# Gate and up projections of feed-forward tiles 3 to 20 as seven block products each

## The chip, the cores and the metric
The kernel runs on one NeuronCore of one Trainium2 chip. The metric is device time in microseconds. Three runs of the kernel before took 2664.05, 2674.93 and 2677.69 us, median 2674.93.

## The reference, cut to what matters
Two equal layers are applied to 576 tokens (512 of a prompt, 64 of a sample). In each layer a feed-forward network stands first and another last; between them are a mixer of four head groups and a cross attention over 256 memory rows.

```
def swiglu(x, w_gate, w_up, w_down):
    return (jax.nn.silu(x @ w_gate) * (x @ w_up)) @ w_down

x = layer_norm(ALPHA * x + 0.5 * swiglu(x, ffn1_gate, ffn1_up, ffn1_down), g[0], b[0])
mix, state = parallel_mixer(x, ...)
x = layer_norm(ALPHA * x + mix, g[1], b[1])
x = layer_norm(ALPHA * x + cross_attention(x, mem_k, mem_v, x_wq, x_wo), g[2], b[2])
x = layer_norm(ALPHA * x + 0.5 * swiglu(x, ffn2_gate, ffn2_up, ffn2_down), g[3], b[3])
```
The model width is 1024, the hidden width 2816. All data is fp32.

## The kernel before
**Precision.** Every operand of a large product is split into a high part (rounded to fp32r, TensorE's one-pass fp32 kind) and a low part (the rest). A product takes three matmuls: high by high, high by low, low by high (`passes`, L394). One matmul is 128 weights columns by 288 tokens, half of the 576, into one PSUM bank. Both halves, h0 and h1, lie in the two banks of a "pair"; the pairs are A, B, D0 and D1.

**Weights.** All weights come as a stream of "units" of 128x1024 (512 KB), in the order of use. SyncE loads them into a ring of three raw buffers. Pool splits each: one TENSOR_SCALAR makes the high part (L2135), four TENSOR_TENSORs the low part (L2142), into one of 12 slots. `unit_split` counts units that are ready, `unit_done` units that TensorE is through with; `SLOT` and `BEFORE` say which slot a unit gets and which unit must be done first. RING is 3, so the load of a unit waits for the split of the unit three before it.

**A feed-forward network** has 22 hidden tiles of 128, each with a gate unit and an up unit, and down units for every two tiles. TensorE goes through it in four stretches:
- The head: tiles 0 to 2, all six units for half h0, then all six for h1 (96 matmuls for four of them and 24 for each of the other two), while the LayerNorm before it is still finishing half h1.
- Tiles 3 to 20: gate of a tile into A, up into B (`proj`, L417, 48 matmuls each); after every odd tile the down product of an earlier pair of tiles (`down`, L542, 8 output tiles of 12 matmuls, in D0 and D1 by turns). Two tiles and a down product make a "half" of six units. Nine halves: the first stands alone, eight are run in a loop of two.
- The tail: tile 21 and the last down products by halves of the tokens (`tail`, L472). Ahead of the up product of h1 stand the first sums of the next LayerNorm (`stats(j, 0)`, L586), for which TensorE waits.

**The other engines** run their own programs in a fixed order and meet by semaphores. ScalarE applies SiLU to the gate (L1099) and makes the high part of the hidden tile (L1103). VectorE multiplies by the up product (L1591), makes the low part (L1595), and adds each down product to y (L1609). Pool, after the last unit of the tail, splits six more units, the first of the next stage (mixer units, or the next layer's head), and only then adds up the squares for the LayerNorm (`squares_sum`, L2157) that `stats` waits for. After the last network of the last layer there are no such six.

Of the kernel before, what the change touches and what calls it, by code (L numbers as in the profile page):

```python
# [74 lines left out]
SLOTS = 12  # L75
HEAD, TAIL, BODY = 6, 6, 12
BODIES = (FFN_UNITS - HEAD - TAIL - 6) // BODY
FFN_H = 6 + 2 + 4 * BODIES + 2


def slot_table():

    table = [(u + 6) % SLOTS for u in range(FFN_UNITS)]
    table += [i if i < HEAD else (i - HEAD) % 5 for i in range(MIX_UNITS + X_UNITS - 3)] + [HEAD - 1, 6, 7]
    table += [u % SLOTS for u in range(FFN_UNITS)]
    last = {s: u - UNITS for u, s in enumerate(table)}
    before = []
    for u, s in enumerate(table):
        before.append(last[s])
        last[s] = u  # L90
    return table, before


SLOT, BEFORE = slot_table()
for at_ in (0, FFN2_AT):
    for u_ in range(at_ + HEAD + 6, at_ + FFN_UNITS - TAIL):
        assert SLOT[u_] == SLOT[u_ - BODY] and BEFORE[u_] == u_ - BODY
# [10 lines left out]
    "pairA_full": 61, "pairA_free": 61, "pairA.0_full": 6, "pairA.0_free": 6, "pairA.1_full": 5, "pairA.1_free": 5,  # L108
    "pairB_full": 47, "pairB_free": 47, "pairB.0_full": 6, "pairB.0_free": 6, "pairB.1_full": 5, "pairB.1_free": 5,
# [4 lines left out]
    "act_step": 77, "stats_ready": 8, "stats_done": 16, "y_done": 64, "mean_sq": 8, "y_summed": 7, "gw_split": 1,  # L114
    "conv": 2, "rows": 1, "rowexp": 2, "c.sq": 2, "a.probs": 12, "a.pv": 10, "b.turned": 4, "b.sq": 2, "x.probs": 5,
    "x.pv": 3, "lam_ln": 1, "lam4": 1, "d.tanh": 2, "d.sqrt": 2, "d.out": 2, "rows_in": 1, "lf_ln": 1, "c.dT": 4,
    "c.abs": 4, "c.rstd": 2, "c.out": 2, "a.nmax": 12, "a.exp": 12, "b.rstd": 2, "b.out": 2, "xq1_hi": 1,
    "x.nmax": 5, "init": 0,
# [16 lines left out]
def build_program(nc, io, counts):  # L135
    made = {}
    with ExitStack() as ctx:
# [19 lines left out]
        w_raw = sb("w_raw", [P, RING, 8, P])  # L157
        w_0 = sb("w_0", [P, 5, 2, 8, P], F32R)
        T = [sb(f"scratch{i}", [P, XPW]) for i in range(6)]
# [5 lines left out]
        gw_raw = sb("gw_raw", [P, KT, 36])  # L165
        gw_hi = sb("gw_hi", [P, KT, 36], F32R)
        gw_lo = sb("gw_lo", [P, KT, 36], F32R)
        lru_w = sb("lru_w", [P, 4, P])
# [33 lines left out]
        with ExitStack() as s:  # L202

            w_6 = sb("w_6", [P, 2, 2, 8, P], F32R, scope=s)
            below_w_8 = sb("below_w_8", [P, 512], scope=s)
            w_8 = sb("w_8", [P, 4, 2, 8, P], F32R, scope=s)
            h_lo2 = sb("h_lo2", [P, 2, TOK], F32R, scope=s)
            below_w_5 = sb("below_w_5", [P, 656], scope=s)
            w_5 = sb("w_5", [P, 2, 8, P], F32R, scope=s)
            h_hi2 = sb("h_hi2", [P, 2, TOK], F32R, scope=s)  # L210
        with ExitStack() as s:
            beside_pa = sb("beside_pa", [P, 14 * TOK], scope=s)
            pt = sb("pt", [P, 2, 2, TP], scope=s)
# [24 lines left out]
        pad2 = sb("pad_s", [P, 7552])  # L238

        slots = [(w_0[:, i, 0], w_0[:, i, 1]) for i in range(5)] + [(w_5[:, 0], w_5[:, 1])]  # L240
        slots += [(w_6[:, i, 0], w_6[:, i, 1]) for i in range(2)] + [(w_8[:, i, 0], w_8[:, i, 1]) for i in range(4)]
# [68 lines left out]
        mean_sq = counted("mean_sq")  # L310
        mem_hi_done, mem_split = sem("mem_hi_done"), sem("mem_split")
# [19 lines left out]
        def inc(ins, c):  # L331
            c.n += 1
            ins.then_inc(c.sem, 1)


        @block.tensor
        def _(pe):
# [7 lines left out]
            with pe.Fori(0, DEPTH) as l:  # L345
# [126 lines left out]
                def tail(u, fi, j, h0, label):  # L472
# [3 lines left out]
                    pairs_read(A, B, D0, D1)  # L476
# [84 lines left out]

                def ffn(fi, u0, x_stage, h0, before, j):
# [1900 lines left out]
```

## Time and profile before
| | us |
|---|---|
| median of three runs | 2674.93 |
| span of the profiled execution | 2675.5 |
| TensorE matmul busy | 2556.2 (96%) |
| weight loads busy | 2444.5 (91%) |
| Pool busy | 1542.6 (58%) |
| VectorE busy | 1056.0 (39%) |
| ScalarE busy | 583.9 (22%) |

The page gives no other time of the profiled execution than its span from the first to the last instruction; it lies 0.6 us above the median. Busy times are of the whole span. TensorE's matmuls overlap by pipelining, so the pace is read from the chain of waits: there a piece of the chain is a run of matmuls with its start, its length and its count.

### The profile page before, as it was taken

How to read it: one execution, taken by the hardware profiler on the slowest of the kernel's cores; microseconds unless marked ns; L12 is line 12 of the kernel's file. 1: busy time of each engine (PE TensorE's matmuls, PEld its weight loads, DVE VectorE, ACT ScalarE, POOL GpSimd, SP SyncE). 2: the span in 40 equal slices, each digit the busy share in tenths (PEclk: the TensorE clock that was granted, in tenths of full speed). 3: DMA queues.
4: the chain of work that ended last, by engine and by line, in shares of the span. 5: the costliest groups of instructions: out<-in, count | busy, mean ns of one | idle time of the engine just before them, and what ended most of it. 6: DMA issues, size and time to landing. Idle time of an engine off the chain costs nothing.

```text
span 2675.5 us, 47942 instructions
## 1 busy us (share of the span) xinstructions
PE 2556.2 (96%) x18450; PEld 2444.5 (91%) x18450; DVE 1056.0 (39%) x1601; ACT 583.9 (22%) x1096; POOL 1542.6 (58%) x1877
## 2 busy tenths in 40 slices
PE   8999999999988899999999999999999879999997
PEld 7999999978767799999999999999787768999997
DVE  3222225654647622222422222256445575222224
ACT  2000004422315500000320000044223254000004
POOL 8866662733239686666486666626332588766641
PEclk9999999989979999999999999999889999999999
DMA  6322220212113132222132222202121121322201
GB/s 229 118 79 86 79 86 9 80 48 71 52 48 95 57 113 81 85 80 84 40 114 87 83 82 80 83 2 87 40 89 35 64 97 64 103 87 78 85 33 36
DMA packets 61099, 203.99 MB, mean 76 GB/s; under 512 B 6808, under 2 KB 13976, under 8 KB 60312
## 3 DMA queue, kind: packets, MB, share of 16 engines
q1 hardware_dynamic: 52288, 184.83, 21.3%
q10 hardware_dynamic: 8664, 17.17, 1.8%
q8 instruction: 96, 1.57, 0.2%
q14 instruction: 51, 0.42, 0.1%
HBM read 195.66 MB, written 7.88 MB: 76 GB/s over the span
## 4 chain that ended last, share of the span: by engine, by line
PE 84%; DVE 9%; POOL 3%; issue 3%; ACT 1%; DMA 0%; DVEq 0%; POOLq 0%; ACTq 0%
PE pairA L401 22%; PE pairD L401 20%; PE pairB L401 19%; PE pairD L410 8%; PE pairA L410 2%; PE pairB L410 2%; POOL scratch L2175 1%; PE pairD L671 1%; PE pairD L673 1%; POOL w L2142 1%; DVE prx L2098 1%; DVE scratch L1816 1%; DVE y L1634 1%; PE pairD L793 0%; PE pairB L828 0%
## 5 line engine op out<-in xcount | busy, mean ns | idle before, releaser
L2142 POOL TENSOR_TENSOR w<-w_raw,w 128x256 fp32r<-128x256 f32 x1372 | 1044.2, 792 | 28.6
L2135 POOL TENSOR_SCALAR w<-w_raw 128x1024 fp32r<-128x1024 f32 x343 | 365.3, 1065 | 808.3 <-issue 450.0
L401 PE MATMUL pairA<-x_hi,w 128*128 128x288 f32 x3136 | 570.3, 299 | 3.6 <-DVE scratch L1564 2.7
L401 PE MATMUL pairB<-x_hi,w 128*128 128x288 f32 x2752 | 497.1, 298 | 0.0
L401 PE MATMUL pairD<-h_hi,w 128*128 128x288 f32 x2688 | 481.0, 298 | 16.0 <-DVE kw L1906 6.3
L401 PEld LDWEIGHTS pairA<-x_hi,w 128*128 128x128 f32 x3136 | 473.9, 191 | 7.0 <-issue 6.1
L401 PEld LDWEIGHTS pairD<-h_hi,w 128*128 128x128 f32 x2688 | 403.8, 191 | 18.9 <-issue 8.4
L401 PEld LDWEIGHTS pairB<-x_hi,w 128*128 128x128 f32 x2752 | 413.9, 191 | 1.1 <-issue 0.2
L1609 DVE TENSOR_TENSOR y<-y,pairD 128x576 f32<-128x576 f32 x256 | 193.1, 754 | 561.6 <-PE pairD L401 561.6
L401 PE MATMUL pairA<-x_lo,w 128*128 128x288 f32 x1568 | 339.1, 298 | 0.0
L401 PE MATMUL pairB<-x_lo,w 128*128 128x288 f32 x1376 | 297.2, 298 | 0.0
L401 PE MATMUL pairD<-h_lo,w 128*128 128x288 f32 x1344 | 290.6, 298 | 0.0
L1103 ACT ACTIVATE h_hi<-scratch 128x576 fp32r<-128x576 f32 x72 | 49.4, 686 | 956.5 <-DVE scratch L1591 956.5
L401 PEld LDWEIGHTS pairA<-x_lo,w 128*128 128x128 f32 x1568 | 256.2, 191 | 0.0
L401 PEld LDWEIGHTS pairB<-x_lo,w 128*128 128x128 f32 x1376 | 223.7, 191 | 0.0
L401 PEld LDWEIGHTS pairD<-h_lo,w 128*128 128x128 f32 x1344 | 218.3, 190 | 0.0
L2175 POOL TENSOR_TENSOR scratch<-scratch 128x288 f32<-128x288 f32 x112 | 98.6, 880 | 192.9 <-ACT scratch L1120 188.9
L410 PE MATMUL pairD<-x_hi,w 128*128 128x288 f32 x832 | 175.7, 303 | 22.0 <-DVE w L1520 12.4
L1591 DVE SCALAR_TENSOR_TENSOR scratch<-scratch,pairB 128x576 f32<-128x576 f32 x72 | 54.0, 751 | 339.8 <-PE pairB L401 339.8
L410 PEld LDWEIGHTS pairD<-x_hi,w 128*128 128x128 f32 x832 | 138.0, 192 | 24.9 <-issue 19.6
L410 PE MATMUL pairD<-h_hi,w 128*128 128x288 f32 x768 | 158.4, 298 | 2.3 <-DVE h_lo L1770 2.3
L410 PEld LDWEIGHTS pairD<-h_hi,w 128*128 128x128 f32 x768 | 124.6, 188 | 4.7 <-DVE h_lo L1770 3.2
(340 smaller groups left out, 2925.0 us busy)
## 6 DMA issues: line engine op xcount, KB each, us to landing
w_raw<-in_stream SPq DMA_DIRECT2D x348, 512.0 KB, 3.4
out_ak<-pa ACTq DMA_DIRECT2D x2, 1152.0 KB, 4.7
out_y<-y SPq DMA_DIRECT2D x8, 288.0 KB, 2.2
mem_raw<-in_mem ACTq DMA_DIRECT2D x2, 1024.0 KB, 4.7
cst<-in_consts ACTq DMA_DIRECT2D x1, 1740.0 KB, 8.2
tb_dram<-in_rel ACTq DMA_DIRECT2D x2, 768.0 KB
y<-in_x ACTq DMA_DIRECT2D x2, 576.0 KB, 7.0
y<-in_x ACTq DMA_DIRECT2D x1, 1152.0 KB, 11.2
```

The lines of the kernel that those rows point to most:

```text
L401: ins.append(mm(out[0:m, half, 0:n], wt, mv_[:, c:c + n], start=(start and i == 0), stop=(stop and i == 2)))
L410: return [mm(out[:, 0:HT], wt, mv_[:, c], start=(start and i == 0), stop=(stop and i == 2)) for i, (wt, mv_) in enumerate(((wh, hi), (wh, ...
L671: i = mm(o[m, cols], lhs, dT[:, h, tok], start=True, stop=(t == 0))
L673: i = mm(o[m, cols], cs[r, p, st, 0:w], qw[r, p, tok], start=False, stop=True)
L1103: f(hs[t % 4][0], hf[:, 0:TOK], ACT.Copy).then_inc(h_hi_done.sem, 1)
L1591: v.scalar_tensor_tensor(out=both(hf[:, 0:TOK]), in0=both(sil[t % 2][:, 0:TOK]), scalar=0.5, in1=B.halves(), op0=ALU.mult, op1=ALU.mult).t ...
L1609: v.tensor_tensor(both(y[:, n]), both(y[:, n]), pair.halves(), ALU.add)\
L1634: v.scalar_tensor_tensor(out=y[:, n, half(h)], in0=y[:, n, half(h)], scalar=scalar, in1=t[:, 0:HT], op0=ALU.mult, op1=ALU.add).then_inc(us ...
L1816: step(v.reciprocal(r_, r_))
L2135: pool.tensor_scalar(hi, w_raw[:, j], 1.0, 0.0, ALU.mult, ALU.add).then_inc(unit_hi, 1)
L2142: i_ = pool.tensor_tensor(lo[:, b], w_raw[:, j, b], hi[:, b].bitcast(F32), ALU.subtract)
L2175: pool.tensor_tensor(s2[:, c], a[:, c], sil[n % 2][:, c], ALU.add)\
```

## The change
For tiles 3 to 20 the gate and the up product of one tile are taken together as a 2x2 by 2x2 block product: the weights as blocks A11 and A12 (gate, lower and upper four of the eight 128-row pieces of the width) and A21, A22 (up), the tokens as halves h0, h1 of the lower and upper pieces. Strassen's scheme in Winograd's form gives the four results from seven products in place of eight:
- Four weight sums per tile, S1 = A21 + A22, S3 = A11 + A21, S2 = S1 + A11, S4 = S2 + A12, are made by VectorE from the raw units. ScalarE makes the high parts of all seven blocks, Pool the low parts of the three raw blocks (A11, A12, A22), VectorE the low parts of the four sums.
- Four token sums, T1 to T4, 128x1152 each, are made once for each network by VectorE in the head, with high parts by ScalarE and low parts by VectorE.
- TensorE runs seven `part`s of 12 matmuls (`tile_pair`), into A0, A1, B0, B1 and then a second time into A0, B0, B1. Between the two, ScalarE copies A0 out, and VectorE combines the products in five additions of 128x288 per tile (`combine`).
- The seven blocks of a tile (two sets, x for odd tiles and y for even ones) and the token sums take the room of the slots. The down units keep two slots. The tail's six units get the blocks e0/e1, the second down slot, and four slots that lie on the token sums; the last four wait for a product of tile 20 in addition.
- The loads of the mixer's gate and recurrence weights are issued in the first tail and no longer in the first network.

Where the blocks and units lie:

```diff
+SETS = (("e0", "e1", "e2", "sc", "b0", "b1", "b2"), ("b3", "b4", "b5", "b6", "b7", "b8", "b9"))
+D_SLOTS, TAIL_SLOTS = (5, 8), (9, 8, 10, 11, 12, 13)
+TAIL_OVER = {62: 2, 63: 3, 64: 4, 65: 7}
...
+    parts = {i: (f"b{2 * i}", f"b{2 * i + 1}") for i in range(5)}
+    parts |= {5: ("d0",), 6: ("t0",), 7: ("t1",), 8: ("d1",), 9: ("e0", "e1")}
+    parts |= {10: ("t0",), 11: ("t1",), 12: ("t2",), 13: ("t3",), "x": SETS[0], "y": SETS[1]}
```

TensorE:

```diff
+                    def part(bank, b, src, start):
+                        (wh, wl), (hi, lo) = blocks[b], src
+                        ins = []
+                        for k in range(4):
+                            for i_, (wt, mv_) in enumerate(((wh, hi), (wh, lo), (wl, hi))):
+                                ins.append(mm(bank.t[:, 0:HT], wt[:, k], mv_[:, k], start=(start and k == i_ == 0),
+                                              stop=(k == 3 and i_ == 2), skip_group_check=not start))
...
+                    unit_there(u + 1, BODY * off)
+                    if not first:
+                        pe.wait_ge(gate_on.sem, at(gate_on, 2, -1))
+                    tell_over(part(A.bank[0], A11, x_[0][0], True))
...
+                    pe.wait_ge(sum_lo.sem, at(sum_lo, 4, 3))
+                    part(A.bank[1], S2, tx[T2], True)
+                    if not first:
+                        pe.wait_ge(combined.sem, at(combined, 5, -1))
+                    part(B.bank[0], S1, tx[T1], True)
+                    if not first:
+                        pe.wait_ge(combined.sem, at(combined, 5, 0))
+                    part(B.bank[1], S3, tx[T3], True)
+                    pe.wait_ge(m1_kept.sem, at(m1_kept, 1, 1))
+                    part(A.bank[0], A12, x_[1][0], False)
+                    pe.wait_ge(sum_lo.sem, at(sum_lo, 4, 4))
+                    pe.wait_ge(combined.sem, at(combined, 5, 2))
+                    part(B.bank[0], S4, x_[1][1], False)
+                    pe.wait_ge(combined.sem, at(combined, 5, 3))
+                    part(B.bank[1], A22, tx[T4], False)
+                    units_over(2)
...
                     head(u0, x_stage, [(x, fi, f) for f in range(3) for x in "gu"], before)
                     banks_read(A, B)
-                    proj(u0 + 6, A, ("g", fi, 3))
-                    proj(u0 + 7, B, ("u", fi, 3))
+                    tile_pair(u0 + 6, 3, fi)
...
-                            proj(u, A, None, 12 * i, 4 * i, a0 + 2 * m)
-                            proj(u + 1, B, None, 12 * i, 4 * i, b0 + 2 * m)
+                            tile_pair(u, 5 + 2 * m, fi, i)
```

VectorE, in the head and in the nine halves:

```diff
                         for t in range(3):
+                            if (h, t) == (0, 2):
+                                tokens_made(fi)
                             hidden_half(fi, t, h)
+                            if (h, t) == (0, 2):
+                                tokens_lo(fi)
+                            if (h, t) == (1, 0):
+                                sums(fi, 3, 0)
+                                sums(fi, 3, 2)
+                            if (h, t) == (1, 1):
+                                for n in range(4):
+                                    sums_lo(fi, 3, n)
...
+                    def half_body(k, off=0):
+                        t, r = 2 * k + 3, 2 * k + 4
+                        more = k + 1 < HALVES
+                        combine(fi, t, h0, 0, off)
+                        combine(fi, t, h0, 1, off)
+                        combine(fi, t, h0, 2, off)
+                        if k:
+                            sums(fi, r, 0, off)
+                        combine(fi, t, h0, 3, off)
+                        if k:
+                            sums(fi, r, 2, off)
+                        combine(fi, t, h0, 4, off)
+                        hidden(fi, t, off)
+                        if k == 0:
+                            hidden_lo(fi, t, h0, off)
+                            sums(fi, r, 0)
+                            sums(fi, r, 2)
+                        for n in range(KT):
+                            down_add(k, n, off)
+                            if n == 1 and k:
+                                hidden_lo(fi, t, h0, off)
+                            if n in (1, 2, 4, 5):
+                                sums_lo(fi, r, (1, 2, 4, 5).index(n), off)
+                        if more:
+                            sums(fi, t + 2, 0, off)
+                        combine(fi, r, h0, 0, off)
```

Pool, a unit's added wait and the order of a half:

```diff
+                    if SLOT[w] in TAIL_SLOTS[2:]:
+                        pool.wait_ge(product.sem, product.value(l, 7 * ((w // FFN2_AT + 1) * PAIRS - 1)
+                                                                + TAIL_OVER[w - w // FFN2_AT * FFN2_AT]))
...
+                    def half_body(k, off=0):
+                        u = at + HEAD + HALF * k
+                        pair_lo(u, fi, 2 * k + 3, off)
+                        unit(u + 2, off)
+                        unit(u + 3, off)
+                        pair_lo(u + 4, fi, 2 * k + 4, off)
```

Three places of the changed order follow. VectorE, in the head of a network, from tile 1 of half h0 to tile 0 of half h1 (tq_f holds the raw token sums, tq their parts, e_0f and scratch raw weight sums). Before:

```order
L1564 SCALAR_TENSOR_TENSOR scratch<-scratch,pairD 128x288 [waits pairD0.1_free,pairD1.1_full,h_ready]
L1571 REGISTER_ALU
L1572 TENSOR_TENSOR h_lo<-scratch,h_hi 128x288 [waits h_hi_done]
L1006 ISA [waits h_ready]
L1011 REGISTER_ALU [waits pairB.0_full]
L1564 SCALAR_TENSOR_TENSOR scratch<-scratch,pairB 128x288 [waits pairA.0_free]
L1571 REGISTER_ALU
L1572 TENSOR_TENSOR h_lo<-scratch,h_hi 128x288 [waits h_hi_done]
L1011 REGISTER_ALU [waits pairD1.0_full,h_ready]
L1564 SCALAR_TENSOR_TENSOR scratch<-scratch,pairD 128x288 [waits pairD0.0_free]
```

Now, from the first token sum to the first product of half h1:

```order
L1779 TENSOR_TENSOR tq_f<-y 128x1152 [waits h_ready]
L1780 TENSOR_TENSOR tq_f<-y 128x1152
L1781 ISA
L1782 TENSOR_TENSOR tq_f<-y,tq_f 128x1152 [waits tx_made]
L1783 REGISTER_ALU
L1784 TENSOR_TENSOR tq_f<-y,tq_f 128x1152 [waits tx_made]
...
L1790 TENSOR_TENSOR tq<-tq_f,tq 128x1152 [waits tx_hi,h_ready]
L1789 REGISTER_ALU
L1790 TENSOR_TENSOR tq<-tq_f,tq 128x1152 [waits tx_hi] x2
L1789 REGISTER_ALU
L1790 TENSOR_TENSOR tq<-tq_f,tq 128x1152 [waits tx_hi]
L1140 REGISTER_ALU [waits pairD1.0_full]
```

Eight operations of 128x1152 stand where none stood, four ahead of tile 2 of h0 and four behind it; sums and low parts of tile 3's weights follow in h1.

VectorE again, around tile 3's hidden product (L1591 before, L1841 now) and the first additions of a down product (L1583 before, L1868 now); w_0f holds tile 4's raw sums. Before, and now:

```order
L1583 SCALAR_TENSOR_TENSOR y<-y,pairD 128x576 [waits pairD0_full]
L1583 SCALAR_TENSOR_TENSOR y<-y,pairD 128x576 [waits pairD1_full]
L1589 ISA
L1590 ISA [waits pairB_full]
L1591 SCALAR_TENSOR_TENSOR scratch<-scratch,pairB 128x576 [waits pairA_free]
L1594 REGISTER_ALU
L1595 TENSOR_TENSOR h_lo<-scratch,h_hi 128x576 [waits h_hi_done]
```

```order
L1847 TENSOR_TENSOR h_lo<-scratch,h_hi 128x576 [waits h_hi_done]
L412 REGISTER_ALU
L416 REGISTER_ALU [waits unit_landed2,unit_landed1]
L1802 TENSOR_TENSOR w_0f<-w_raw 128x512 [waits unit_done]
L1803 TENSOR_TENSOR w_0f<-w_raw 128x512
L1805 REGISTER_ALU
L1806 TENSOR_TENSOR w_0f<-w_0f,w_raw 128x512 [waits sum_made]
L1807 REGISTER_ALU
L1808 TENSOR_TENSOR w_0f<-w_0f,w_raw 128x512 [waits sum_made]
L1135 ISA
L1868 SCALAR_TENSOR_TENSOR y<-y,pairD 128x576 [waits pairD0_full]
```

Before, the additions of the down product stood ahead of tile 3's hidden product; now they stand behind it, its low part and the four sums of tile 4.

Pool, from the third unit of the tail (the first two before it wait for `unit_landed` and `unit_done` as ever). Before, and now:

```order
L2135 TENSOR_SCALAR w<-w_raw 128x1024 [waits unit_landed2,unit_done]
L2142 TENSOR_TENSOR w<-w_raw,w 128x256 [waits unit_hi]
L2142 TENSOR_TENSOR w<-w_raw,w 128x256 x3
L2135 TENSOR_SCALAR w<-w_raw 128x1024 [waits unit_landed0,unit_done]
L2142 TENSOR_TENSOR w<-w_raw,w 128x256 [waits unit_hi]
```

```order
L2450 TENSOR_SCALAR t<-w_raw 128x1024 [waits product,unit_landed2,unit_done]
L2457 TENSOR_TENSOR t<-w_raw,t 128x256 [waits unit_hi]
L2457 TENSOR_TENSOR t<-w_raw,t 128x256 x3
L2450 TENSOR_SCALAR t<-w_raw 128x1024 [waits product,unit_landed0,unit_done]
L2457 TENSOR_TENSOR t<-w_raw,t 128x256 [waits unit_hi]
```

The slots t are the token sums' room, and each of the four such units waits for a product of tile 20. The order of units and of the squares behind them is the same: six units of the next stage stand between the tail's units and the squares.

## Rows read from the trace of the kernel before

**Rows 1.** The page: busy time, and TensorE's granted clock by slices.
```profile
PE 2556.2 (96%) x18450; PEld 2444.5 (91%) x18450; DVE 1056.0 (39%) x1601; ACT 583.9 (22%) x1096; POOL 1542.6 (58%) x1877
PEclk9999999989979999999999999999889999999999
```

**Rows 2.** Chain of waits, a half of the loop, head and tile 3: start us, us, what.
```profile
290.57 6.40 PE pairB L401 x48
296.97 12.80 PE pairD L401 x96
...
928.20 12.80 PE pairD L410 x96
948.27 6.62 PE pairA L401 x48
```

**Rows 3.** Stretch 290 to 385 us: length, busy PE, PEld, DVE, ACT, POOL, clock, DMA.
```profile
290.00:385.00 95.00, 95.00 (x716) 95.00 (x715) 24.35 (x31) 6.00 (x9) 60.08 (x75) 1.00 0.26 83
```

**Rows 4.** Single VectorE and ScalarE lines: min/median/max ns.
```profile
L1591 DVE SCALAR_TENSOR_TENSOR scratch<-scratch,pairB x72: 746/751/755, 80.3 to 2618.0; 128x576 f32<-128x576 f32 x72
L1595 DVE TENSOR_TENSOR h_lo<-scratch,h_hi x72: 758/1180/1324, 81.8 to 2619.5; 128x576 fp32r<-128x576 f32 x72
L1572 DVE TENSOR_TENSOR h_lo<-scratch,h_hi x32: 457/604/1050, 33.5 to 2647.6; 128x288 fp32r<-128x288 f32 x32
L1079 ACT ACTIVATE h_hi<-scratch x32: 442/445/447, 33.0 to 2647.1; 128x288 fp32r<-128x288 f32 x32
L1103 ACT ACTIVATE h_hi<-scratch x72: 682/686/692, 81.1 to 2618.8; 128x576 fp32r<-128x576 f32 x72
```

**Rows 5.** Timeline, VectorE and Pool streaming from SBUF together at 11 us.
```profile
11.82 7.62 DVE L1525 TENSOR_TENSOR x_lo<-y,x_hi 128x576 fp32r<-128x576 f32 x6
...
10.91 5.19 POOL L2142 TENSOR_TENSOR w<-w_raw,w 128x256 fp32r<-128x256 f32 x4
```

**Rows 6.** Timeline of VectorE in the head at 928 us.
```profile
927.68 0.60 DVE L1572 TENSOR_TENSOR h_lo<-scratch,h_hi 128x288 fp32r<-128x288 f32 x1 [0.51 <-ACT h_hi L1079]
934.79 0.45 DVE L1564 SCALAR_TENSOR_TENSOR scratch<-scratch,pairD 128x288 f32<-128x288 f32 x1 [4.88 <-ACT scratch L1075]
```

**Rows 7.** Timeline and chain, two other heads: last low part of tile 1, half h1.
```profile
35.37 0.60 DVE L1572 TENSOR_TENSOR h_lo<-scratch,h_hi 128x288 fp32r<-128x288 f32 x1 [0.51 <-ACT h_hi L1079]
...
33.68 9.75 PE pairD L410 x73
...
1359.17 0.81 DVE L1572 TENSOR_TENSOR h_lo<-scratch,h_hi 128x288 fp32r<-128x288 f32 x1 [0.51 <-ACT h_hi L1079]
...
1364.43 12.80 PE pairD L410 x96
```

**Rows 8.** Chain of waits, first tail: start us, us, what.
```profile
400.59 3.40 PE pairA L410 x24
...
423.04 0.48 PE pairA L606 x2
```

**Rows 9.** Timeline of Pool: squares in the first tail, and units back to back.
```profile
413.81 0.81 POOL L2175 TENSOR_TENSOR scratch<-scratch 128x288 f32<-128x288 f32 x1 [8.35 <-ACT scratch L1120]
...
420.96 0.81 POOL L2175 TENSOR_TENSOR scratch<-scratch 128x288 f32<-128x288 f32 x1 [0.74 <-ACT scratch L1120]
...
474.28 1.05 POOL L2135 TENSOR_SCALAR w<-w_raw 128x1024 fp32r<-128x1024 f32 x1
475.42 2.82 POOL L2142 TENSOR_TENSOR w<-w_raw,w 128x256 fp32r<-128x256 f32 x4
478.20 1.05 POOL L2135 TENSOR_SCALAR w<-w_raw 128x1024 fp32r<-128x1024 f32 x1
```

**Rows 10.** TensorE's waits at 1290 to 1365 us, stretches, and the run behind.
```profile
PE pairD L410 <- POOL w L2142: 3.4, 1, 3.4
...
1344.00:1348.00 4.00, 4.00 (x19) 4.00 (x18) 3.56 (x5) 3.79 (x7) 4.00 (x5) 0.50 0.31 120
...
1342.75 15.37 PE pairD L410 x96
```

## What the change does to the time: a prediction

> **What bounds the kernel now.** I read the page first [rows 1]: TensorE is busy 96% of the span, Pool 58%, VectorE 39%, and the granted clock is full almost everywhere. The chain of waits then shows the loop over tiles 3 to 20: gate, up and down follow one another without a gap, 48 matmuls in 6.40 us and 96 in 12.80, which is 133.3 ns each [rows 2]. The stretch of 95 us in that loop says the same, with the clock at 1.00, that is 2.4 GHz [rows 3]. So in the loop only the number of matmuls counts, as long as nobody else is late. Between the loops (head, tail, LayerNorm) TensorE meets the others, and there an in-order queue decides. The span, 2675.5 us, is 0.6 us above the median of the runs; I take the sum against it.
>
> **What goes.** A tile needs 7 x 12 = 84 matmuls in place of 96. Eighteen tiles, two networks, two layers: 72 x 12 = 864 matmuls less, x 133.3 ns = **115.2 us**. The shape and the number of weight loads per matmul stay, so I keep the pace. The rest of the work is to find how much of it is given back.
>
> **Durations I use.** VectorE, 288 columns alone 0.46 us, 576 alone 0.76 [rows 4]: 1.045 ns a column, so 512 columns cost 0.69 and 1152 cost 1.36, some 0.08 less each in a run. With an operand in PSUM, 576 always cost 0.75 [rows 4], also beside Pool. With both in SBUF it is otherwise: the low part of a hidden tile takes 1.18 in the median and up to 1.32, and a run of six beside a streaming Pool took 7.62 us, 1.27 each against 0.68 alone, while Pool's four took 5.19 and not 2.82 [rows 4, 5, 9]. So when both stream from SBUF, a VectorE operation costs 0.6 more, and Pool is held up as much. ScalarE: 0.445 for 288, 0.686 for 576 [rows 4], so 0.64 for 512 and 1.17 for 1152. Pool: a unit alone follows the one before in 3.92 us [rows 9].
>
> The Trainium skill (SBUF — State Buffer, section "SBUF: two separate sides") says more: VectorE with two SBUF inputs and GpSimd hold a shared port pair by an exclusive lock for a whole instruction, and the other "fully blocks". By that rule each operation in a run would wait out a whole Pool operation, 0.70 and not 0.6; the terms below that hold twelve such operations a network would grow by 1.2 us each, 5 us in all, and the sum would be 2699.
>
> **Step 1, the head.** Take the second network of layer 0 and count from the start of h1 on TensorE, 928.20 [rows 2]. VectorE ends the low part of tile 1 at 0.1 [rows 6]. Four token sums take it to 5.5, tile 2's product to 6.0. ScalarE is behind its four token copies until 6.7, then makes that tile's high part (7.15); low part 7.6. Four low parts of the token sums, 5.1: 12.7. Only then comes tile 0 of h1, which began at 6.6 before [rows 6]: product, high, low part end at 14.15. The four weight sums of tile 3 cost 2.6 alone and 5.0 beside Pool, which starts on its low parts now: 19.1. ScalarE's copy of the last and its SiLU take it to 20.2, tile 1's product, high and low part to 21.6. Four low parts of the sums, again 5.0 at most, 4.2 as Pool is not there all the time: 25.8. Tile 2's product frees bank B1: 26.3, and TensorE starts 0.3 later at 26.6. Before, tile 3 started at 948.27, that is 20.1 [rows 2]. **Late by 6.5.** With nothing contended the same chain ends at 23.1, late by 3.0. The last network is alike. In the first network VectorE is free at 2.3 and not 0.1 [rows 7], late by 8.7; in layer 1's first it is free at -4.4 [rows 7] and the chain ends 4.5 earlier, late by 2. Sum 23.7, bounds 11 and 34.
>
> **Step 2, the first down product.** Let T be the end of tile 3. Last combination T+0.7, hidden product +1.5, high part +2.2, low part +3.0. Now come the four sums of tile 4, beside Pool again: +8.0 (+5.6 alone). Only then the first addition, +8.7, and TensorE, which has two pairs and needs the first one back at T+3.2, goes on at +9.0. **5.8 a network, 23.2 in all**, bounds 13.5 and 26.
>
> **Step 3, the other halves.** A half is 264 matmuls, 35.2 us. VectorE has in it 8 additions (0.70), 8 sums (0.64), 8 low parts of sums (0.69), 10 combinations (0.46), 2 hidden products and 2 low parts (0.76): 23.9 us alone. Pool's TENSOR_TENSORs fill 14 of the 35 us, so 20 SBUF operations x 0.4 x 0.6 = 4.8: 28.7, or 81%. The down product is its tightest place: pieces n = 4 and 5 hold an addition and a low part, 1.45 alone, 1.9 beside Pool, against 1.6 for TensorE's twelve matmuls. Two pairs of banks absorb most. I take 0.4 a half for seven halves and 1.3 for the last, where Pool splits the first tail unit at the same time: 4.1 a network, **16**. Bounds 1 and 38. The products' own waits have slack: a bank is wanted back 3 us or more after its product ends, and a combination takes 0.46. Pool's and ScalarE's work per half (about 18 and 11 us) fits.
>
> **Step 4, the tail.** This is the largest. Before, the slots let Pool run up to twelve units ahead, and after its last unit it waited 8.35 us for the first square [rows 9]. Now the second unit of the tail waits for the end of the last down product, and the next four for products of tile 20. Let X be the start of tile 20. Pool starts at X+0.4 and has eleven units in a row (five of the tail, six of the next stage): 3.95 + 10 x 3.92 = 43.2, so X+43.6, with 2.5 for VectorE's operations beside it X+46. Seven additions of squares at 0.8 (0.81 each [rows 9]): X+51.7. TensorE wants the sum at X + 11.2 (tile 20) + 1.0 + 22.4 (from the tail's start to `stats`, 400.59 to 423.04 [rows 8]) = X+34.6. **It waits 17.2 us, in three of the four tails: 51.6.** All that follows hangs on this sum, so nothing of it is won back. Without contention it is 14.7 each, 44; with the worst 19, 57. The tail's own units are in time (the fourth is wanted at X+18.6 and ready at X+16).
>
> **Step 5, the clock.** After an idle time of 3.4 us TensorE's clock stood at 0.50, 1.2 GHz, and 96 matmuls took 15.37 us instead of 12.80: 2.6 us [rows 10]. Steps 1, 2 and 4 make ten idle times longer than that (3 + 4 + 3). At 2.1 each, since the clock need not fall at the shorter ones: **21**, bounds 8 and 27.
>
> **Small.** The tail starts 0.8 earlier, as the last hidden product no longer reads PSUM; the moved loads cost ScalarE 0.8 in two tails: together -2.
>
> **Sum.** -115.2 + 23.7 + 23.2 + 16 + 51.6 + 21 - 2 = +18.3. 2675.5 + 18.3 = **2694 us**. Slower by 0.7%: the matmuls saved are given back by four waits outside the steady loop.
>
> **Rivals.**
> *A: VectorE and Pool hardly meet in the new order.* ScalarE's copies pace Pool's low parts, so the two could fall between each other. For it speaks the lowest low part, 0.758 [rows 4]; against it, the median, 1.18, and that sums and Pool's parts are set off by the same arrival. With lone durations the steps are 12, 13.5, 3, 45, 14 and -2: 85.5, or 2646. It decides the sign where the extra per operation falls from 0.6 under about 0.2. This is the case of not slower, 20%.
> *B: VectorE bounds the steady halves.* At 81% busy, an added wait of 0.1 us at each of some forty operations would push the additions late, and the banks D0 and D1 with them; 1.2 us a half and not 0.4 gives 28 x 0.8 + 13 = 35 more: 2729. Against it: before, VectorE idled more than half of the loop [rows 3], and each stretch outside the down product has slack. 15%.
> *C: the backlog of step 4 isn't there,* because Pool's work ahead of it is done early enough, or the sum is wanted later than I read. Then step 4 and its clock go: 2694 - 51.6 - 6 = 2636. Against it stands the order: the four waits for tile 20 are in Pool's queue ahead of the squares. 10%.
> The forecast's case holds 55%, by itself 2670 to 2715.
>
> **Chances.** What a measurement tells from no change is about 0.5%, 13 us. Faster by more: C and most of A, and a little of the forecast: 0.27. Within: the lower part of the forecast and the rest of A: 0.25. Slower by more: 0.48. The bounds of the terms give 2633 to 2742 at the ends; 8 in 10 I put between 2640 and 2736.
>
> **What would show it.** In the loop, seven groups of 12 matmuls a tile, 1.60 us each, and halves of 35.2 to 35.8 us. Step 1: tile 3 of the second network starts 26 to 27 us after its h1 and waits for VectorE; at 20 it is wrong. Step 2: a gap of 5 to 6 us after two pieces of the first down product only. Step 4: TensorE idle 15 to 19 us ahead of the first average of the next LayerNorm, released by Pool, in three tails and not in the fourth; Pool's units without a gap from tile 20 on. Step 5: the clock at half behind these gaps. A steady half above 36.5 us would be B. The forecast as a whole is wrong if Pool waits for ScalarE's squares in the first tail, as it did before.

## The result

Median 2660.2 us (2647.5 to 2672.2), against 2673.2 us for the kernel before beside it (2664.1 to 2680.8), 15 runs of each. The ratio is 0.9964, with a 95% interval of 0.9947 to 0.9980: faster by 0.36%. That is less than the 0.5% that the prediction took for the smallest change to be told, but the interval lies clear of 1. The forecast was 2694 us, slower by 0.7%. So the sign was wrong, and the sum was too high by some 24 to 31 us, by which of the measures below one takes.

The page of the profile after, which answers to [rows 1]:
```profile
span 2670.3 us, 49634 instructions
PE 2463.7 (92%) x17586; PEld 2343.7 (88%) x17586; DVE 1707.9 (64%) x2569; ACT 924.1 (35%) x1760; POOL 1413.9 (53%) x1589
PEclk9999998988989999999899999989889799999999
```
The 864 matmuls are gone, but TensorE fell from 96% to 92% of the span: it now waits. The run that the page shows took 2672.2 us, 12 above the median. The second mixer in it took 5.9 us more than before, with the granted clock at 0.92 (before 0.94). The matmuls there are the same in both kernels, and the kernel before itself has 0.92 in its first mixer and 0.94 in its second, so I don't count that part as the change's.

TensorE's waits after (waiting line, releaser: us in total, times, longest):
```profile
PE pairA L735 <- POOL scratch L2517: 57.5, 11, 18.0
PE pairD L487 <- DVE y L1868: 19.5, 4, 4.9
PE pairA L666 <- DVE scratch L1761: 16.9, 4, 7.1
PE pairA L496 <- DVE scratch L1834: 3.7, 4, 0.9
PE pairD L487 <- DVE y L1874: 1.2, 4, 0.3
```
In their order these are step 4 (three of 18 and eight short ones), step 2, step 1, the start of the tail, and all that is left of step 3. The last row is the surprise: 1.2 us where 16 were forecast. Its four waits of 0.3 us all stand in the last half of a network, where Pool splits the first unit of the tail; the 28 halves between the first and the last have none.

The chain of waits shows the steady half (start us, us, what), which answers to [rows 2], and the stretch of it by engines (length, busy PE, PEld, DVE, ACT, POOL, clock, DMA) to [rows 3]:
```profile
291.07 12.74 PE pairD L487 x96
...
326.12 12.73 PE pairD L487 x96
```
```profile
291.07:326.12 35.05, 35.05 (x266) 35.05 (x266) 26.50 (x39) 11.63 (x23) 20.74 (x22) 1.00 0.27 90
```
Two down products follow each other in 35.05 us, 38.4 before, and TensorE is busy without a gap. VectorE is busy 26.5 us of it, 76%; the forecast had 28.7 and 81%.

The chain through the first tail, which answers to [rows 8, 9]:
```profile
374.78 1.06 POOL d L2450
...
400.54 3.58 POOL w L2457 x4
...
426.10 0.80 POOL scratch L2517
...
427.02 1.32 PE pairA L735 x2
```
Pool starts its eleven units at 374.78 and ends the last square at 426.9. In the forecast's count from X, the start of tile 20 (here 374.4), that is X+0.4 and X+52.5, where X+0.4 and X+51.7 stood. TensorE was ready at 409.1, X+34.7, and waited 17.95 us.

### The profile page after: what moved, and what is told of

The parts are those of the page before. It is cut to its first block, busy times and chain, and to the rows that moved or that the text cites. A ratio compares the mean times of both kernels' runs of the same rounds, so it can differ in the third digit from the quotient of the medians.

```text
span 2670.3 us, 49634 instructions
## 1 busy us (share of the span) xinstructions
PE 2463.7 (92%) x17586; PEld 2343.7 (88%) x17586; DVE 1707.9 (64%) x2569; ACT 924.1 (35%) x1760; POOL 1413.9 (53%) x1589
## 4 chain that ended last, share of the span: by engine, by line
PE 71%; DVE 12%; POOL 7%; issue 6%; ACT 3%; ACTq 0%; DMA 0%; DVEq 0%; POOLq 0%; SPq 0%
PE pairD L487 19%; PE pairB L666 17%; PE pairA L666 13%; PE pairA L487 5%; PE pairD L496 4%; POOL w L2457 3%; PE pairB L487 2%; POOL scratch L2517 2%; PE pairB L496 1%; PE pairD L800 1%; PE pairD L802 1%; POOL t L2457 1%; PE pairA L496 1%; POOL w L2450 1%; DVE prx L2412 1%
## 5 line engine op out<-in xcount | busy, mean ns | idle before, releaser
L2474 POOL TENSOR_TENSOR w<-w_raw,w 128x256 fp32r<-128x256 f32 x360 | 311.2, 890 | 334.5 <-DVE w_0f L1808 307.6
L2457 POOL TENSOR_TENSOR w<-w_raw,w 128x256 fp32r<-128x256 f32 x556 | 471.0, 877 | 11.6
L2450 POOL TENSOR_SCALAR w<-w_raw 128x1024 fp32r<-128x1024 f32 x139 | 147.8, 1063 | 384.6 <-issue 380.2
L487 PE MATMUL pairD<-h_hi,w 128*128 128x288 f32 x1536 | 289.5, 306 | 35.6 <-DVE y L1868 19.5
L487 PEld LDWEIGHTS pairD<-h_hi,w 128*128 128x128 f32 x1536 | 240.0, 198 | 39.8 <-DVE y L1868 20.5
L666 PE MATMUL pairB<-tq,w 128*128 128x288 f32 x1728 | 247.4, 295 | 0.0
L666 PEld LDWEIGHTS pairB<-tq,w 128*128 128x128 f32 x1728 | 235.9, 188 | 0.0
L487 PE MATMUL pairD<-h_hi,d 128*128 128x288 f32 x1152 | 206.1, 295 | 1.2 <-DVE y L1874 1.2
L666 PE MATMUL pairA<-x_hi,w 128*128 128x288 f32 x864 | 188.1, 294 | 0.0
L487 PEld LDWEIGHTS pairD<-h_hi,d 128*128 128x128 f32 x1152 | 171.1, 188 | 2.2 <-DVE y L1874 2.1
L496 PEld LDWEIGHTS pairD<-x_hi,w 128*128 128x128 f32 x832 | 137.5, 192 | 25.6 <-issue 20.1
L487 PE MATMUL pairA<-x_hi,w 128*128 128x288 f32 x832 | 156.2, 306 | 0.0
L666 PEld LDWEIGHTS pairA<-x_hi,w 128*128 128x128 f32 x864 | 143.9, 188 | 0.0
```

Of the source, the lines that this page charges most:

```text
L487: ins.append(mm(out[0:m, half, 0:n], wt, mv_[:, c:c + n], start=(start and i == 0), stop=(stop and i == 2)))
L496: return [mm(out[:, 0:HT], wt, mv_[:, c], start=(start and i == 0), stop=(stop and i == 2)) for i, (wt, mv_) in enumerate(((wh, hi), (wh, ...
L666: ins.append(mm(bank.t[:, 0:HT], wt[:, k], mv_[:, k], start=(start and k == i_ == 0), stop=(k == 3 and i_ == 2), skip_group_check=not start))
L2450: pool.tensor_scalar(hi, w_raw[:, j], 1.0, 0.0, ALU.mult, ALU.add).then_inc(unit_hi, 1)
L2457: i_ = pool.tensor_tensor(lo[:, b], w_raw[:, j, b], hi[:, b].bitcast(F32), ALU.subtract)
L2474: i_ = pool.tensor_tensor(lo[:, c], src[:, c], hi[:, c].bitcast(F32), ALU.subtract)
```

## The experiments

Nine kernels, grouped by the wait that they bear on. All change the kernel after, unless said otherwise. The ratios are to the kernel before, and the savings are the 0.9964 of after less the ratio, times 2671.

**Pool's squares ahead of the next stage's units.**
```diff
-                units(mix, mix + HEAD)
+                unit(mix)
                 squares_sum(0, 0)
+                units(mix + 1, mix + 5)
                 squares_sum(0, 1)
-                units(mix + HEAD, cross - 5)
+                units(mix + 5, cross - 5)
```
(and the same for the second network)

> The changed kernel, but Pool adds up the squares behind one of the six units of the next stage (squares of half 0, four units, squares of half 1, the sixth unit), where it made all six first. Theory 'queue': the three waits of 18 us ahead of the first average are Pool's backlog of next-stage units and nothing else. The tail's own units end at about 395.5 in the first network, one more unit 399.4, seven additions at 0.8 us: 407.3, and TensorE wants the sum at 409. So the three waits go to under 1 us, 53 us less, and with the half-speed clock behind them (2 us each) about 59: 2660 - 59 = 2601. Rival 'squares': ScalarE's squares or the tail's additions are late too, now that VectorE and the tail's slots are tighter; then 5 us or more stays in each tail, released by ScalarE, and the time is 2615 to 2625. Rival 'pays back': the next stage's units come late, and 5 us or more turns up where the next stage begins (2615 or more).

Ratio 0.9809 (0.9773 to 0.9845), 41 us less than after. The 18 us waits are gone, so the backlog was Pool's order. But only 41 of 59 came, and the rival "pays back" has its part: TensorE now waits at the mixer's first unit, in the first and third network 4.4 us and not 1.7 and 1.5. Pool's timeline there, and the row of ScalarE behind it (start us, us, line, operation, what, idle before and its releaser):
```profile
422.15 3.57 POOL L2457 TENSOR_TENSOR w<-w_raw,w 128x256 fp32r<-128x256 f32 x4
425.68 1.32 POOL L2517 TENSOR_TENSOR scratch<-scratch 128x288 f32<-128x288 f32 x1
427.56 1.85 POOL L2517 TENSOR_TENSOR scratch<-scratch 128x288 f32<-128x288 f32 x2 [0.55 <-ACT scratch L1315]
```
```profile
427.04 0.78 ACT L1315 ACTIVATE scratch<-y 128x288 f32<-128x288 f32 x2 [3.27 <-POOL scratch L2517]
```
The first square of half 1 has no idle time before it: it had been waiting behind four units. ScalarE, which has two buffers for squares, stood in turn behind it for 3.27 us, with the copies of x that TensorE needs.

**The same move in the kernel before**, as a control.

> The kernel before, with the same move of Pool's squares as in the run sq_first. In it Pool had waited 8.35 us for the first square, so there was no backlog. Theory 'queue': no change (within 0.3%), and no wait of TensorE at the averages of the next LayerNorm. Rival: if the move itself saved time whatever the slots (because the sums came earlier than they are asked for), this kernel would be faster by 10 us or more.

Ratio 1.0077 (1.0052 to 1.0102): slower by 20 us. I had expected no change, and both expectations fell. The trace:
```profile
414.17 0.81 POOL L2175 TENSOR_TENSOR scratch<-scratch 128x288 f32<-128x288 f32 x1 [42.28 <-ACT scratch L1120]
...
439.12 1.32 POOL L2175 TENSOR_TENSOR scratch<-scratch 128x288 f32<-128x288 f32 x1
```
In the kernel before, Pool makes the next stage's units early, all but the last inside the loop and that one at 401 us. With the squares moved ahead of them it idles 42.28 us for the first square and makes four units just when the squares of half 1 come; the first of these starts at 439.12, in the kernel before at 433.88. TensorE waits 4.3 and not 1.4 us at the mixer, with the clock at half behind it. From the tail's start to that point it is 3.5 us in the first network. The whole profile is 18.3 us longer than that of the kernel before. In it the three tails up to that point hold some 11 us. Another 7 lie in the first mixer, which took 493.6 us and not 486.7; some 3 of these are the low clock behind the wait, and whether the rest has to do with the move, one trace doesn't tell. The control shows that the price of an order is that of the backlog it meets: the same lines cost 20 us in one kernel and gave 41 in the other.

**The squares of half 1 one unit earlier** (`units(mix + 1, mix + 4)`, squares, `units(mix + 4, ...)`).

> The changed kernel; Pool makes one unit of the next stage, the squares of half 0, three units, the squares of half 1, and two units (in the run sq_first four units stood ahead of the squares of half 1). Theory 'blocked': in sq_first the first square of half 1 was taken at 425.68 behind four units, where ScalarE had it ready some 5 us before; ScalarE's queue stood behind it with the copy of x, and TensorE waited 4.4 us instead of 1.7 at the mixer's first unit. With three units the squares begin at about 421.7: that wait goes back to 1.5 us and the clock stays up behind it, some 3 to 6 us less in each of three tails: 2620 - 12 = 2608. Rival 'late units': the two last units now come late and TensorE waits for Pool in the mixer's first units; then 2620 or more.

Ratio 0.9760 (0.9731 to 0.9789), median 2606.5: 54 us less than after, and 13 less than in the first experiment. The three tails up to the next stage's first unit are 8 us shorter than there; what lies behind is mixed with the clock of the mixers. The wait at the mixer is 1.97 us. "Blocked" holds, and no wait for the late units shows.

**The first down product** (`sums` now makes one sum at a call).
```diff
-                        if k == 0:
-                            hidden_lo(fi, t, h0, off)
-                            sums(fi, r, 0)
-                            sums(fi, r, 2)
                         for n in range(KT):
                             down_add(k, n, off)
+                            if k == 0:
+                                if n < 4:
+                                    sums(fi, r, n // 2 * 2, which=(n % 2,))
+                                else:
+                                    sums_lo(fi, r, n - 4)
+                                if n == KT - 1:
+                                    hidden_lo(fi, t, h0, off)
+                                continue
```


> The changed kernel, but in the first half the four weight sums of tile 4 stand one behind each of the first four additions of the down product, the low parts of the sums behind the other four, and the low part of tile 3's hidden product last, where all of it but the low parts of the sums stood ahead of the first addition. Theory 'queue': the gap of 4.9 us after two pieces of the first down product is only this order. It goes to under 0.5 us, four times: 18 us less, and the clock that was at half behind it gives 2 us a network back: 2660 - 26 = 2634. Rival 'load': VectorE has 8 x 0.75 + 8 x 0.7 to 1.1 + 0.8 = 13 to 15.6 us of work in a product of 12.8, so 1 to 3 us stay, spread over the pieces or ahead of tile 4's second product; 2642 to 2650.

Ratio 0.9852 (0.9822 to 0.9883), median 2635.2: 30 us less. The four waits of 4.9 us don't appear any more, and none of over 0.2 us has come in their place. "Queue" holds, "load" doesn't.

**The order in the head.**
```diff
                             if (h, t) == (0, 2):
-                                tokens_lo(fi)
+                                tokens_lo(fi, ((2, T2),))
 ...
                             if (h, t) == (1, 1):
-                                for n in range(4):
+                                for n in range(3):
                                     sums_lo(fi, 3, n)
+                            if (h, t) == (1, 2):
+                                tokens_lo(fi, ((0, T1), (1, T3)))
+                                sums_lo(fi, 3, 3)
+                                tokens_lo(fi, ((3, T4),))
```
(TensorE waits for each token sum at the product that reads it)

> The changed kernel, but in the head VectorE makes the low parts of three of the four token sums and of the fourth weight sum only behind the last hidden product, each just ahead of the product that reads it; before, all stood ahead of it. Theory 'work in line': tile 3 waits because VectorE has 4.5 us of low parts too many ahead of the product that frees the last bank. The waits of 7.15, 4.47 and 4.47 us go to about 2.7, 0.9 and 0.9, the third (0.8) stays: 11.6 us less, with the clock about 16: 2644. Rival 'elsewhere': the same work then holds up products 2, 3 and 6 of tile 3 or tile 3's combinations, and 3 us or more of it comes back there; 2652 or more.

Ratio 0.9902 (0.9868 to 0.9936), 17 us less. The waits are 2.77, 0.73, 0.81 and 0.73 us, as "work in line" has it; 0.3 us comes back at tile 3's sixth product in three of the four networks.

**Contention taken away.** Pool's low parts of the raw blocks are left out, but for one small operation a tile, and TensorE reads the high part in their place:
```diff
                         for k in range(0, 4, 2):
 ...
+                            if (n, k) != (2, 2):
+                                continue
```


> The changed kernel without Pool's low parts of the three raw blocks of each tile (of the six operations one stays, on 64 columns, for the counters; TensorE reads the high part in the place of the low one, so its work is the same). VectorE then has Pool beside it only while Pool splits the down product's two units. Theory 'small': contention with these low parts costs VectorE some 2 us a half and TensorE nothing in the steady halves; what goes is only their share in the head and the first down product: the four weight sums at tile 3 cost 0.68 and not 1.2, so the waits of 4.47 at tile 3 fall by about 2, and those of 4.9 at the first down product to about 2.9: 14 to 18 us with the clock, 2643 to 2648. The forecast's price (0.6 us on every one of twenty operations a half) would give 4.1 us a network more. Halves stay at 35.06.

Ratio 0.9871 (0.9841 to 0.9901), some 25 us less (21 by the medians). The waits, and a steady half in this run (the row by stretches again):
```profile
PE pairD L487 <- DVE y L1870: 11.5, 4, 2.9
PE pairA L668 <- DVE scratch L1763: 10.5, 4, 4.8
```
```profile
284.85:319.91 35.06, 35.06 (x267) 35.06 (x266) 25.03 (x39) 11.54 (x23) 11.11 (x12) 1.00 0.25 90
```
Both terms fall, from 19.5 and 16.9 to 11.5 and 10.5 us, and the half stays at 35.06. So what this contention costs shows in the head and in the first down product; "small" holds, with somewhat more than its 14 to 18 us. (The forecast had put its price on 0.4 of the twenty operations, not on every one.) In a steady half it costs VectorE 1.5 us and TensorE nothing.

**Four more VectorE operations a half, in the down product** (one in a network's first half).
```diff
+                            if k and n in (1, 2, 4, 5) or (k, n) == (0, KT - 1):
+                                more_work(fi, k, (1, 2, 4, 5).index(n) if k else -1, n, off)
```


> The changed kernel with four more VectorE operations in each steady half, 128x512 with both inputs in SBUF (y added to itself into a scratch tile nobody reads), all in the down product, behind its additions 1, 2, 4 and 5. VectorE's share of a half goes from 26.5 of 35.06 us (76%) to about 84%. Theory 'place': what counts is how far VectorE runs behind within the pieces. An addition, a low part and the new operation cost 0.67 + 0.60 + 0.67 = 1.94 against 1.6 a piece, with the hidden tile's low part 2.6 at the first; it falls 1.35 behind against 0.75 of slack, so TensorE waits 0.3 to 0.6 us a half: halves of 35.4 to 35.7, 10 to 18 us in all. Theory 'share' (the one on which the forecast put 0.4 us a half at 81%): at 84% 0.8 to 1.2 us a half, 22 to 34 us in all.

**The same four between the combinations of the two tiles.**

> The same four VectorE operations a half, but between the combinations of the two tiles. Same share of VectorE, 84%. Theory 'place': VectorE idles 0.4 to 1.2 us ahead of most combinations and a bank is wanted back 3 us after its product, so TensorE never waits: halves of 35.06 us, no change. Theory 'share': the same 0.8 to 1.2 us a half as with the load in the down product.

One run of each: 2721.1 and 2693.8 us. Their spans are 49 and 22 us above that of the profile after, and the four loops hold 46 and 13 of it. Waits of the first, then a half of each by stretches:
```profile
PE pairD L488 <- DVE y L1883: 29.8, 60, 1.4
```
```profile
232.62:268.96 36.34, 35.59 (x264) 35.13 (x264) 29.44 (x43) 11.56 (x23) 20.87 (x23) 1.00 0.24 87
```
```profile
225.03:260.61 35.58, 35.34 (x265) 35.11 (x265) 31.47 (x43) 11.64 (x23) 22.37 (x22) 1.00 0.24 89
```
In the down product the load costs 1.28 us a half with VectorE at 81%; between the combinations 0.52 us a half with VectorE at 88%. Neither theory's numbers hold. "Place" is right in that the place counts for more than the share (the lower share costs more), but it was too low for both, and zero between the combinations is refuted: the load there makes the first addition of the down product late. "Share" is refuted by the order of the two. As these are single runs, I read the halves of their traces, where the clock is at 1.00, and not the times.

**All three orders together.**

> The three orders together: Pool's squares as in sq_later, the first down product as in down_first, the head as in head_order. Theory 'independent': the three waits stand in different stretches and each is set by its own queue, so the savings add: against 2660, 53.7 (sq_later), 25.0 (down_first) and 12.7 (head_order) make 91, so 2569; no wait of TensorE over 3 us is left in the feed-forward parts, and halves stay at 35.06 us. Rival 'overlap': the clock's half speed behind these waits is one loss that the three share, or tile 4's work moved into the down product meets the head's moved low parts on VectorE; then less than 80 us in all, 2580 or more.

Ratio 0.9602 (0.9577 to 0.9628), median 2563.4: 4.0% faster than before, 97 us less than after, where the three savings make 101. "Independent" holds, but for one wait of 3.4 us at the head of layer 1, which stood there before the change too. It is the fastest of all kernels here. From the page and the waits of this run:
```profile
PE 2435.2 (95%) x17586; PEld 2323.7 (91%) x17586; DVE 1723.6 (67%) x2569; ACT 925.3 (36%) x1760; POOL 1440.8 (56%) x1589
```
```profile
PE pairD L496 <- DVE y L1966: 5.9, 6, 2.0
PE pairA L666 <- DVE scratch L1767: 5.0, 4, 2.8
```

## Why the prediction was wrong

Term by term, waits and stretches of the two profiles, us:

| step | forecast | measured | from |
|---|---|---|---|
| 864 matmuls | -115.2 | -118.1 | the four loops, their waits and low clock taken off |
| 1, head | +23.7 | +13.3 | 16.9 of waits, less the 3.6 that stood there before |
| 2, first down product | +23.2 | +19.5 | its row of waits |
| 3, other halves | +16 | +1.2 | its row of waits |
| 4, tail | +51.6 | +53.9 | 17.95, 18.04, 17.95 |
| 5, clock | +21 | +20.1 | half of the time at the lower level behind ten gaps |
| small | -2 | -1.8 | waits at the tail's start 0.93, not 1.37 |
| sum | +18.3 | -11.9 | |

The 0.36% of the timed runs is -9.6 us. The two spans differ by -5.2; +6.6 of that lies in the mixers, so the parts that the table covers differ by -11.8. The sum of the forecast was thus 30 us too high there: 15 in step 3, 10 in step 1, 4 in step 2, 3 in the matmuls, and step 4 was 2 too low.

**The gain** was right in kind and 3 us too small. In the run with all three orders the second network's loop takes 318.0 us from tile 3 to the tail (915.59 to 1233.61), before 346.8: 28.8 a network, 216 x 133.3 ns. But some short waits are left in that loop. With waits and low clock taken off, the loops of after are 29.5 shorter, for TensorE's pace did not quite stay: a half of 264 matmuls takes 35.05, which is 132.8 ns each.

**Step 3 is the one that failed.** It took Pool to be beside VectorE for 0.4 of the time, spread that evenly over 20 operations, the down product with the rest, and put 0.4 us of waiting on each half, for which it gave no working. The number contended was about right, eight of the 20 in this half; their places were not. The rows of a down product on VectorE after show where Pool is not:
```profile
294.28 0.75 DVE L1874 TENSOR_TENSOR y<-y,pairD 128x576 f32<-128x576 f32 x1 [0.81 <-PE pairD L487]
294.95 0.75 DVE L1847 TENSOR_TENSOR h_lo<-scratch,h_hi 128x576 fp32r<-128x576 f32 x1
295.62 0.68 DVE L1816 TENSOR_TENSOR w<-w_0f,w 128x512 fp32r<-128x512 f32 x1
...
296.89 0.69 DVE L1816 TENSOR_TENSOR w<-w_0f,w 128x512 fp32r<-128x512 f32 x1
...
299.73 1.08 DVE L1816 TENSOR_TENSOR w<-w_0f,w 128x512 fp32r<-128x512 f32 x1
...
303.85 0.76 DVE L1874 TENSOR_TENSOR y<-y,pairD 128x576 f32<-128x576 f32 x1 [0.84 <-PE pairD L487]
...
316.61 1.22 DVE L1816 TENSOR_TENSOR w<-w_0f,w 128x512 fp32r<-128x512 f32 x1
317.75 1.29 DVE L1847 TENSOR_TENSOR h_lo<-scratch,h_hi 128x576 fp32r<-128x576 f32 x1
```
```profile
291.45 0.74 POOL L2474 TENSOR_TENSOR w<-w_raw,w 128x256 fp32r<-128x256 f32 x1 [1.78 <-DVE w_0f L1808]
297.00 1.87 POOL L2474 TENSOR_TENSOR e<-w_raw,e 128x256 fp32r<-128x256 f32 x2 [4.81 <-ACT e L1225]
298.83 2.58 POOL L2474 TENSOR_TENSOR w<-w_raw,w 128x256 fp32r<-128x256 f32 x3
308.95 0.74 POOL L2474 TENSOR_TENSOR w<-w_raw,w 128x256 fp32r<-128x256 f32 x1 [7.55 <-DVE w_0f L1808]
```
An operation of 128x512 takes 0.68 us alone and 1.1 to 1.3 when Pool holds it up. The price, 0.4 to 0.6, was near the forecast's. Three of the down product's four low parts take 0.68 or 0.69 (the fourth stands at 301.40, as Pool stops). For the one at 296.89 it is Pool that pays, with 1.87 us for two operations and not 1.4. Pool waits 4.81 us for ScalarE's copies there, streams for 4.4 us, and waits again for 7.55. Its long run, from 309 to 325, falls on the combinations, where VectorE had 0.4 to 1.2 us to spare ahead of most. So VectorE idles 0.8 us ahead of three of the eight additions in the tightest place, and TensorE never waits. With the load brought to that very place a half does lose time, 1.28 us; so contention in that place could have cost what the step said, but no run here puts it there.

**Step 1** failed for the same reason, in part. The second network after:
```profile
951.76 1.11 DVE L1808 TENSOR_TENSOR w_0f<-e_0f,w_raw 128x512 f32<-128x512 f32 x1
...
955.48 0.69 DVE L1816 TENSOR_TENSOR e<-e_0f,e 128x512 fp32r<-128x512 f32 x1
...
957.29 0.68 DVE L1816 TENSOR_TENSOR w<-w_0f,w 128x512 fp32r<-128x512 f32 x1
957.89 0.45 DVE L1761 SCALAR_TENSOR_TENSOR scratch<-scratch,pairB 128x288 f32<-128x288 f32 x1
```
```profile
949.99 4.17 POOL L2474 TENSOR_TENSOR w<-w_raw,w 128x256 fp32r<-128x256 f32 x4
```
The weight sums cost 1.1 to 1.2 each, as said; but Pool ended at 954.2, and the four low parts behind took 2.4 us and not 4.2. TensorE started tile 3 at 958.58, 23.7 us after h1 (934.92 as the forecast counts it), where 26.6 was forecast: 1.8 of the 2.9 us is this, and 0.9 that VectorE began the token sums earlier than I had it (934.09). By networks the step measured 6.2, 3.6, -0.1 and 3.6 us where 8.7, 6.5, 2 and 6.5 stood. The chain itself, and its release by tile 2's product, was as described, and moving four low parts behind that product took 11.9 of the 16.9 us away.

**Steps 2 and 4** were right in place, releaser and number of times. In step 2 the four sums did run beside Pool, at 1.1 to 1.23 us each; it was 0.9 us a network too high because the chain ahead of them and they themselves ended somewhat earlier. In step 4 "nothing of it is won back" was right, and the 18 us are all Pool's order.

**Step 5** was right in size. By stretches, behind the waits of 4.47 (twice), 4.89 and 17.95 us:
```profile
958.58:964.00 5.42, 5.42 (x26) 5.42 (x27) 0.46 (x1) 0.65 (x2) 4.54 (x6) 0.60 0.00 2
980.00:984.00 4.00, 4.00 (x18) 4.00 (x19) 1.93 (x4) 0.00 (x0) 0.56 (x1) 0.57 0.52 182
2287.68:2292.50 4.82, 4.82 (x26) 4.82 (x27) 0.46 (x1) 0.65 (x2) 3.95 (x6) 0.68 0.01 3
```
```profile
427.02:433.05 6.03, 6.03 (x30) 5.46 (x31) 2.76 (x5) 1.44 (x4) 0.00 (x0) 0.71 0.00 0
```
The clock is at its lower level, 1.2 GHz, for part of each. All ten gaps were followed by such a stretch, which cost 1.5 to 3.1 us each: also those of 4.5 us, which the forecast had partly spared. Behind the one wait of 0.8 us at tile 3 there was none.

**The rivals.** A was nearest in size (2646), and half of its mechanism is what the rows show: ScalarE's copies do pace Pool's low parts, so that they miss the down product and the end of the head. Its 12 and 3 us for steps 1 and 3 are nearer to the 13.3 and 1.2 measured than the forecast's 23.7 and 16. For the rest it was wrong: VectorE and Pool do meet, at full price in step 2, where its 13.5 stands against 19.5, its 45 for step 4 stands against 53.9, and taking most of the contention away gave 21 to 25 us, not the 48 between A and the forecast. B fell: steady halves of 35.05 us. C fell: the backlog is there. One slip of the prediction's sums: its bounds add up to 2636 and 2740, where 2633 and 2742 stood; nothing hangs on it.

## What to carry to other kernels

When an engine gets close to full, don't spread contention over a period as a mean: list which operations of the two engines stand beside each other, and charge only those, in the place with the least slack. When buffers are made tighter, look for an engine that used to run far ahead; its queue was written for that, and work that somebody waits for may stand behind work that nobody needs yet. And before giving such a change up as even, write the queues anew: the same change was worth 0.4% in its first order and 4.0% with three orders moved, and not one matmul or vector operation less.

## What the runs showed of the hardware

- A short wait costs TensorE more than the idle time shown. In the run with the load in the down product two waits of 0.18 and 0.57 us lengthened the half by 1.28; in the other, one of 0.24 lengthened it by 0.52. That is 0.26 to 0.28 us more for each. It is worked out from single runs. Whether it is the pipeline's filling or the way the ends of matmuls are modelled stays open.
- VectorE beside Pool, both inputs in SBUF: 128x512 took 0.68 us alone and up to 1.31 beside it, and four of Pool's 128x256 took 4.27 and not 2.82 us. The Trainium skill (SBUF — State Buffer, section "SBUF: two separate sides") has the second wait out the whole instruction of the first. The rows agree that each holds the other up, but the 0.63 us that it added at most is less than the 0.70 of Pool's instruction.
- Removing most of Pool's low parts left TensorE's pace as it was (35.06 us a half): no cost of Pool's traffic to it shows.
